# The opening of a two-layer retention and attention kernel: conditioning in four row tiles, filler products, blocks in passes, new tile orders

## What is computed

```python
def _modulation(cond, ada_w, ada_b):
    m = jax.nn.silu(cond) @ ada_w + ada_b
    return jnp.split(m[:, None, :], 6, axis=-1)

def _layer(x, cond, mixer, ...):
    sh1, sc1, ga1, sh2, sc2, ga2 = _modulation(cond, ada_w, ada_b)
    h = _rmsnorm(x, g_pre_mix) * (1.0 + sc1) + sh1
    mixed, side = mixer(_split_proj(h, w_in))      # h @ w_in, 3584 columns
    x = x + ga1 * _rmsnorm(mixed @ w_out, g_post_mix)
    h = _rmsnorm(x, g_pre_ffn) * (1.0 + sc2) + sh2
    x = x + ga2 * _rmsnorm(_conv_ffn(h, w_up, conv_w, conv_b, w_down), g_post_ffn)
    return x, side
```

## Time and profile before

| | |
|---|---|
| three timed runs | 1601.09, 1603.74, 1604.45 us, median 1603.74 |
| span of the profiled execution | 1601.0 us (no time beside its span is recorded for it) |
| TensorE busy | 1575.8 us, 98% |
| VectorE busy | 1275.6 us, 80% |
| ScalarE busy | 794.1 us, 50% |
| GpSimd busy | 379.2 us, 24% |
| DMA | 195.04 MB, mean 122 GB/s |

### The profile page before, as it was taken

One profiled execution on the slowest core, in us unless ns is written; L12 is line 12 of the kernel. 1 busy time (PEld: TensorE's weight loads), 2 busy tenths in 40 slices (PEclk: granted clock), 3 DMA queues, 4 the chain that ended last, 5 costly groups with the idle time before them and its releaser, 6 DMA issues.

```text
span 1601.0 us, 28310 instructions
## 1 busy us (share of the span) xinstructions
PE 1575.8 (98%) x9688; PEld 1389.2 (87%) x9688; DVE 1275.6 (80%) x2255; ACT 794.1 (50%) x1483; POOL 379.2 (24%) x302
## 2 busy tenths in 40 slices
PE   8999999999999999999999999999999999999998
PEld 6788898689999999888878889967899999998886
DVE  7876677968999999966669556987689999998575
ACT  5433235638655565533383323274766565563333
POOL 0031033001455455200000400700035455541000
PEclk9999999999999999999999999999999999999999
DMA  9343265361222222454414414736312222335451
GB/s 369 122 132 111 74 222 179 95 168 55 66 81 89 79 92 79 148 168 158 152 40 145 138 54 134 260 107 146 79 64 82 80 91 79 92 92 178 125 184 66
DMA packets 65494, 195.04 MB, mean 122 GB/s; under 512 B 15361, under 2 KB 16769, under 8 KB 65153
## 3 DMA queue, kind: packets, MB, share of 16 engines
q1 hardware_dynamic: 50114, 175.54, 35.1%
q10 hardware_dynamic: 15296, 18.39, 3.5%
HBM read 187.05 MB, written 6.85 MB: 121 GB/s over the span
## 4 chain that ended last, share of the span: by engine, by line
PE 84%; DVE 7%; issue 2%; ACT 2%; DMA 1%; ACTq 1%; DVEq 0%; SPq 0%
PE bank L2087 14%; PE bank L2088 13%; PE bank L2089 13%; PE bank L2597 10%; PE bank L2599 10%; PE bank L2598 10%; DMA raw<-in_stream 1%; PE bank L2393 1%; PE bank L2457 1%; PE bank L2455 1%; PE bank L2453 1%; PE bank L2380 1%; PE bank L2109 1%; DVE w_lo L1354 1%; PE bank L2277 1%
## 5 line engine op out<-in xcount | busy, mean ns | idle before, releaser
L778 ACT ACTIVATE w_hi<-raw 128x1024 fp32r<-128x1024 f32 (+1 forms) x120 | 123.1, 1029 | 389.0 <-PE bank L2089 325.1
L1354 DVE TENSOR_TENSOR w_lo<-raw,w_hi 128x1024 fp32r<-128x1024 f32 (+1 forms) x128 | 156.3, 1228 | 162.4 <-ACT w_hi L778 162.2
L2087 PE MATMUL bank<-w_hi,aT_lo 128*128 128x512 f32 x520 | 210.5, 405 | 2.1 <-DVE aT_lo L1787 2.0
L2088 PE MATMUL bank<-w_lo,aT_hi 128*128 128x512 f32 x520 | 206.0, 396 | 0.0
L2089 PE MATMUL bank<-w_hi,aT_hi 128*128 128x512 f32 x520 | 205.6, 395 | 0.0
L2597 PE MATMUL bank<-aT_hi,w_lo 128*128 128x322 f32 x640 | 199.8, 312 | 4.5 <-DVE u L1953 4.5
L2598 PE MATMUL bank<-aT_lo,w_hi 128*128 128x322 f32 x640 | 199.4, 312 | 0.0
L2599 PE MATMUL bank<-aT_hi,w_hi 128*128 128x322 f32 x640 | 198.6, 310 | 0.0
L1252 ACT ACTIVATE w_hi<-raw 128x512 fp32r<-128x512 f32 x200 | 117.8, 627 | 105.8 <-POOL raw L660 105.8
L2087 PE MATMUL bank<-w_hi,m_lo 128*128 128x512 f32 x400 | 158.5, 396 | 0.0
L2088 PE MATMUL bank<-w_lo,m_hi 128*128 128x512 f32 x400 | 157.3, 393 | 0.0
(11 more groups left out here) (287 smaller groups left out, 3865.9 us busy)
## 6 DMA issues: line engine op xcount, KB each, us to landing
raw<-in_stream SPq DMA_DIRECT2D x304, 512.0 KB, 3.6
lead<-in_lead SPq DMA_DIRECT2D x16, 512.0 KB, 10.6
bias<-in_bias ACTq DMA_DIRECT2D x8, 896.0 KB, 10.3
na_v<-vn ACTq DMA_DIRECT2D x2, 1280.0 KB, 5.6
x<-in_xs SPq DMA_DIRECT2D x4, 512.0 KB, 12.4
vt<-na_v ACTq DMA_DIRECT2D x16, 128.0 KB
gb_mix<-gates ACTq DMA_DIRECT2D x2, 1024.0 KB, 6.2
gb_ffn<-gates ACTq DMA_DIRECT2D x8, 256.0 KB, 4.5
```

Source lines behind the costliest of these rows:

```text
L778: act.activation(w_hi[:, g % 4, 0:n], raw[:, s % 4, 0:n], ACT.Copy).then_inc(hi_done, 1)
L1354: dve.tensor_tensor(w_lo[:, g % 4, 0:n], raw[:, s % 4, 0:n], w_hi[:, g % 4, 0:n].bitcast(F32), ALU.subtract).then_inc(raw_free[s % 4], 1)
L2087: pe.matmul(out, ll, rh, start=start, stop=False)
L2088: pe.matmul(out, lh, rl, start=False, stop=False)
```

## The change

Ten edits, all in the opening:

- `cond_row` becomes four rows in partitions 0, 32, 64 and 96, loaded by four DMAs; `ones` becomes 128 x 128; the four products take their operands from those partitions.
- `keep_clock` is new: a float32 product of `ones` (128 x 128) with a column of ones repeated 512 times, into bank 5, which nobody reads. It stands at five places.
- Column 3 goes from VectorE to TensorE.
- TensorE's list: columns 0 and 1, column 2, transposes of tile 0, column 3, with fillers between; the transposes of tile 1 directly ahead of the first block; columns 4 and 5 after the first two blocks.
- `lead_block` goes through each quarter in passes: two products high x high, two high x low, two low x high, each pass with its own wait.
- ScalarE loads the table of the square root before its first use (a dummy `Sqrt`), and takes aT_hi of tile 0 ahead of xl of tile 1.
- VectorE has a new order of row scales, columns and low parts.
- `par` (biases and gains, 256 KB) is loaded ahead of the last four lead tiles of the first group.
- The counts of `mod_done` follow from these.
- `low_pass` (line 2142), called by the new block, has the two products of aT_lo and w_hi.

```diff
-LEAD_PE = (0, 1, 2, 4, 5)
-LEAD_DVE = (8, 9, 10, 11, 3, 12, 13, 14, 6, 15, 7)
+LEAD_PE = (0, 1, 2, 3, 4, 5)
+LEAD_DVE = (8, 9, 10, 11, 12, 13, 14, 6, 15, 7)
+LEAD_MOD = (3, 7)
...
-                cond_row = sb("cond_row", [1, 2 * D], F32, s2)
-                ones = sb("ones", [1, P], F32, s2)
+                cond_row = sb("cond_row", [P, W], F32, s2)
+                ones = sb("ones", [P, P], F32, s2)
...
-        mod_done = counted("mod_done", 5, 0, 6)
+        mod_done = counted("mod_done", 5, 0, LEAD_MOD[1] - 2)
...
-            sp_.dma_start(cond_row[:], t["cond"]).then_inc(cond_in, 16)
+            for i in range(4):
+                sp_.dma_start(cond_row[32 * i:32 * i + 1, :], t["cond"][:, i * W:(i + 1) * W]).then_inc(cond_in, 16)
             sp_.dma_start(cond_T[:], t["cond_T"]).then_inc(cond_T_in, 16)
             for i in range(4):
                 column(0, i)
             tokens(0)
             sp_.dma_start(ident[:], t["ident"]).then_inc(ident_in, 16)
+            sp_.dma_start(par[:], t["par"]).then_inc(gains_in, 16)
             for i in range(4, KD):
                 column(0, i)
             sp_.wait_ge(primed, 1)
             tokens(1)
             weight(0)
-            sp_.dma_start(par[:], t["par"]).then_inc(gains_in, 16)
             weight(1)
...
             act.wait_ge(primed, 1)
+            act.activation(prime[:, 15:16], eps[:], ACT.Sqrt)
...
             split_hi(0, 0)
+            lead_high(0, 0)
             lead_scaled(1)
-            lead_high(0, 0)
             split_hi(1, 0)
...
-                dve.tensor_tensor(mod[:, mine, :], mod[:, mine, :], bias(mine), ALU.add).then_inc(mod_done, 1)
+                if mine.stop > mine.start:
+                    dve.tensor_tensor(mod[:, mine, :], mod[:, mine, :], bias(mine), ALU.add).then_inc(mod_done, 1)
...
-            for n in range(4):
+            for n in range(3):
                 lead_products(n)
             row_scale(0, 0, 0)
-            lead_products(4)
-            row_scale(0, 1, 0)
+            lead_products(3)
             lead_mod(0)
             lead_modulate(0, 0)
+            row_scale(0, 1, 0)
             split_lo(0, 0)
             lead_low(0, 0)
             lead_modulate(0, 1)
             split_lo(1, 0)
+            lead_low(0, 1)
             row_scale(0, 2, 0)
-            lead_low(0, 1)
+            lead_products(4)
+            row_scale(0, 3, 0)
             lead_products(5)
-            row_scale(0, 3, 0)
+            lead_low(0, 2)
             lead_products(6)
+            row_scale(0, 4, 0)
+            lead_low(0, 3)
             lead_products(7)
-            lead_low(0, 2)
-            row_scale(0, 4, 0)
             lead_products(8)
-            lead_low(0, 3)
+            lead_low(0, 4)
             lead_products(9)
-            lead_products(10)
-            lead_low(0, 4)
             lead_mod(1)
...
-                pe.wait_ge(norm_lo, NT * h + tt + 1)
+                out = bank[in_bank(0, tt)][:]
+                pe.wait_ge(norm_hi, NT * h + tt + 1)
                 for q in (2 * h, 2 * h + 1):
+                    if tt == 0:
+                        pe.wait_ge(hi_done, q + 1)
+                    for kk in range(2):
+                        k = 2 * q + kk
+                        pe.matmul(out, aT_hi[:, k, toks(tt)], w_hi[:, q, kk * W:(kk + 1) * W], start=k == 0, stop=False)
                     if tt == 0:
                         pe.wait_ge(*freed(stream_of(q), 0))
                     for kk in range(2):
                         k = 2 * q + kk
-                        i_ = mm3(bank[in_bank(0, tt)][:], aT_hi[:, k, toks(tt)], aT_lo[:, k, toks(tt)],
-                                 w_hi[:, q, kk * W:(kk + 1) * W], w_lo[:, q, kk * W:(kk + 1) * W],
-                                 k == 0, k == KD - 1)
+                        pe.matmul(out, aT_hi[:, k, toks(tt)], w_lo[:, q, kk * W:(kk + 1) * W], start=False, stop=False)
+                    pe.wait_ge(norm_lo, NT * h + tt + 1)
+                    i_ = low_pass(tt, q)
...
-            pe.wait_ge(cond_in, 16)
+            pe.wait_ge(cond_in, 64)
+            def keep_clock():
+
+                pe.matmul(bank[5][:], ones[:], ones[:, 0:1].to_broadcast([P, W]), start=True, stop=True)
+
             for i in range(4):
-                pe.matmul(bank[i][:], ones[:], cond_row[:, i * W:(i + 1) * W], start=True, stop=True).then_inc(cond_rows, 1)
+                row = slice(32 * i, 32 * i + 1)
+                pe.matmul(bank[i][:], ones[row, :], cond_row[row, :], start=True, stop=True).then_inc(cond_rows, 1)
+            keep_clock()
+            keep_clock()
             pe.wait_ge(cond_silu, 1)
-            lead_columns(range(3))
+            lead_columns(range(2))
+            keep_clock()
+            lead_columns((2,))
             pe.wait_ge(ident_in, 16)
             lead_transposes(0, 0)
-            lead_transposes(0, 1)
+            keep_clock()
+            lead_columns((3,))
+            keep_clock()
             for tt in range(NT):
+                if tt == 0:
+                    lead_transposes(0, 1)
                 lead_block(0, tt)
                 if tt < 2:
-                    lead_columns((3 + tt,))
+                    lead_columns((4 + tt,))
```

More of the change, by code:

```diff
@@ L1044, in lead_modulate @@
                 act.wait_ge(norm_tp, NT * h + tt + 1)
-                act.wait_ge(mod_done, 4 * h + 4)
+                act.wait_ge(mod_done, LEAD_MOD[h])
                 if tt >= 2:
@@ L1762, in lead_mod @@
                 dve.wait_ge(gains_in, 16)
-                dve.tensor_tensor(mod[:, mine, :], mod[:, mine, :], bias(mine), ALU.add).then_inc(mod_done, 1)
+                if mine.stop > mine.start:
+                    dve.tensor_tensor(mod[:, mine, :], mod[:, mine, :], bias(mine), ALU.add).then_inc(mod_done, 1)
                 dve.tensor_tensor(mod[:, sc, :], mod[:, sc, :], bias(sc), ALU.add).then_inc(mod_done, 1)
-                dve.wait_ge(mod_done, 4 * h + 2)
+                dve.wait_ge(mod_done, LEAD_MOD[h] - 2)
                 dve.scalar_tensor_tensor(mod[:, sc, :], mod[:, sc, :], 1.0,
@@ L1775, in lead_modulate @@
                 dve.wait_ge(norm_tp, NT * h + tt + 1)
-                dve.wait_ge(mod_done, 4 * h + 4)
+                dve.wait_ge(mod_done, LEAD_MOD[h])
                 for a in range(HALF_K):
```

## The result

The changed kernel takes 1609.61 us in the median of five runs (1606.4 to 1610.34), the kernel before 1603.74. The ratio is 1.0036, 95% interval 1.0026 to 1.0047: slower by 5.9 us in the medians, 4.2 to 7.5 by the interval. The forecast was 1603.1; rival A (slower, 1612.2) had the sign and, in the profiled execution, the mechanism. The profiled execution took 1609.9 us, 1.8 above its span.

The account below looks back on a forecast made before the run. TensorE, busy 98% of the span, was taken as the bound, so only an earlier start of dense work could win. Block (1,0) -0.4 and a covered wait -0.2 gave -0.6 us, 1603.1; own range 1601.5 to 1605, whole range 1600.3 to 1612.2.

Parts of the forecast that it names:

- rival A: Opening: TensorE's clock level does not rise until the blocks; block 0 starts at 34.0, +8.5 us, 1612.2; chance 0.21.
- Conditioning: Opening's first products in four row tiles: first starts at 3.7 us, they take 4.3, end at 8.0 instead of 9.6.
- five slots: Conditioning: time taken for four overlapping pairs of records, 4.3 us, with bounds 1.7 and 6.8.
- Fillers: `keep_clock` products in the opening: five take 5.2 us if the first two raise the clock level, 8.5 if it stays low.
- With the level raised at 11.4 to 12: Opening, TensorE at its upper clock: column 3 ends at 21.2, block 0 starts at 24.9, TensorE 1.5 us ahead.
- The forecast's case: Opening: fillers raise the clock level before the columns, giving 1603.1 us; chance 0.45.
- Columns: Column 3 on TensorE: 3.47 us at lower level, about 1.85 at upper; lead tile 4 lands 14.1, xl 0 starts 16.6.
- What is late next: VectorE between modulations of tiles (0,0) and (1,0): 22.5 us of work plus 3.0 of waits, half a microsecond later.
- Passes: Opening blocks: block (1,0) uses aT_hi from 49.0, 0.4 us gained; last wait of 0.2 us covered.
- B: Opening: clock level rises late or falls back during the columns; +3.9 us on the forecast, 1607.0; chance 0.14.
- C: Conditioning: row tiles run one after the other, products end at 10.5; +2.1 us on the forecast, 1605.2; chance 0.08.
- D: Opening: DMA delay not felt, new orders close VectorE's and ScalarE's waits; at most -5.7 us, -3.4 taken, 1600.3; chance 0.12.

Follow-up runs that it names:

- e2: Changed kernel with six float32 fillers right behind the conditioning and none later; 1605.23 us, one run.
- e3: Changed kernel with six fillers behind the conditioning, each four fp32r products, none later; 1608.46 us, one run.
- e9: The changed kernel run again, unchanged; 1609.66 us, ratio 1.0036 to the kernel before.
- e5: Changed kernel with six fillers behind the conditioning plus the change's three later ones; 1613.97 us, ratio 1.0070 to the kernel before.
- e8: Kernel before with row tiles, passes and two fillers where TensorE waits, around the transposes of tile 0; 1601.02 us, ratio 0.9987.
- e1: Changed kernel without its five fillers; 1607.56 us, ratio 1.0022 to the kernel before.
- e7: Changed kernel without fillers and with column 3 back on VectorE; 1604.26 us, ratio 1.0007 to the kernel before.
- e6: Kernel before with conditioning in four row tiles and blocks in passes, old orders, no fillers; 1600.95 us, ratio 0.9982.
- e4: Kernel before with only the conditioning in four row tiles and four DMAs; 1602.56 us, ratio 0.9994.
- e11: Kernel before with row tiles and passes, one strided DMA instead of four for the conditioning row; 1597.96 us, ratio 0.9967.

## Why the prediction was wrong, point by point

*Conditioning: right in direction, missed in size.* Four products in 2.03 us, where I took 4.3. Four records start by 3.3 and the other four between 4.0 and 4.3, so the first records of all four run side by side, then the second ones; my five slots came from a row with two tiles. The Trainium skill (TensorE: Matmul & The Clock Gate, Part 3) gives 3.07 times for four row tiles, an estimated 2.2 us; the trace agrees roughly, with 6.8 over 2.03, 3.4 times. The first product started at 3.25, not 3.7: three issues cost 0.8 us. VectorE's partner product went at 7.76.

*Fillers: the step that failed.* "With the level raised at 11.4 to 12": in the first profiled execution it was not raised before block 0. The prediction's own row against it, 5.7 us of dense products before the rise, was the better evidence: with six fillers it rose 5.1 to 5.3 us into them (e2, e3), and behind two it rose in one profiled execution (e9) and not in the other. The second half of that step failed outright: that the level, once up, stays up through columns. It fell in every profile that had it early (e2, e3, e5, e8, e9), so the fillers, priced as paid back by the clock, cost 4.3 us of opening against e1 (3.5 by e9's profile). The forecast's case did not occur in any profile.

*Columns.* Lead tile 4 was in use at 13.48 against 14.1 said, xl 0 at 15.97 against 16.6. Column 3 was to take 1.85 us at the upper level or 3.47 at the lower: it took 3.41, and with three fillers around it, it ended at 26.6 instead of 21.2. VectorE waited 7.9 us.

*What is late next.* The 1.9 us wait for aT_lo of tile 3 was there, 1.91. But I priced the new orders at half a microsecond beside the old ones; e7 against e6 makes them 4.2 in the opening. The prediction had the piece, xl of tile 1 behind the first modulation, and did not compare it with a kernel that keeps the old order and has the passes. Its own sum of VectorE's list, 22.5 us, is what e6 needs, with no wait.

*Passes.* They were taken at 0.2 us plus a few tenths. e6 against e4 is 3.5 us of opening: block 0 starts before w_lo 0 and aT_lo 0 exist, and no opening block of e6 waits for a low part. In e8 one did, 1.2 us.

*Where it was lucky.* These last two errors, 3.5 us of passes and 4.2 of orders, nearly cancel: row tiles, passes and new orders together (e7) move the opening by +0.1 us, where the forecast had -0.6 for the whole change. That the two come this close is chance. Most of the 6.9 us by which the opening missed is the fillers (4.3) and column 3 (1.8).

*Rivals.* A was right, with its point (columns at 0.21) to the letter; its 34.0 for block 0 was 30.9, mostly because its conditioning ended at 8.0 instead of 5.3. Its +8.5 was +6.3 in the opening and +5.9 in the median. Its chance of 0.21 was too low, since its evidence stood in rows and the forecast's in none. B's sign, column products at two paces, came in e9's profile, but not with its time. C is out. D's 5.7 as the limit of the gain was fair: e11 has 4.35 of it, without the new orders.

The ledger of the opening, us, from one profiled execution each and in the order in which the parts were added: row tiles -0.5, passes -3.5, new orders +4.2, column 3 on TensorE +1.8, fillers +4.3: +6.3 in all. By the ratios of the times the same steps are -1.0, -1.9, +4.0, +2.4 and +2.3, each uncertain by about 2 us: +5.8.

## What to carry to other kernels

A filler is worth its place only if the level it raises survives until the dense work comes, and if the dense work then has its operands. Before you price its gain, read from a profile what the level does in the stretch between. A change of five parts that costs 6 us can contain two that gain 4: build it up from the kernel before, part by part. Passes by operand, with the wait for the late operand last, cost nothing here (a block without a wait takes 2.85 us in e6, 2.87 before) and covered the waits of a split format.

## What the runs showed that was not expected

- In these profiles the granted clock shows nothing before the first rise and reads 1.00 until then: e2 shows 0.50 from 17.2 us, while the same column pace (0.21 us per record) in the changed kernel's 8.85 to 15.5 us stands under 1.00. Use the pace of a known product.
- The level did not rise in 10.4 us of column products without a gap, and in e2 it fell in the middle of them, 4.2 us after the last filler.
- The same code need not have the same level: behind two fillers the columns went at 0.12 us per record in the profiled execution of e9 and at 0.21 in that of the first set. In e1 and e6 the rise came 3.4 and 3.6 us into the first block, in the kernel before 5.7. And the level can fall in a wait of TensorE of 2.4 us: it did in e5 and e9 ahead of block (1,0), and did not in the same wait of the first profile or of e1 and e2.
